# Output products by column halves, TensorE's program written out, sample's transfers in four parts

## The chip, the cores and the metric

The kernel runs on one core of one Trainium2 chip. Of the core's engines, TensorE (PE) multiplies matrices, VectorE (DVE) and ScalarE (ACT) work on rows, GpSimd (POOL) helps at the start, and SyncE (SP) issues most of the transfers; ACT issues some as well. Sixteen DMA engines move the data. The metric is the device time of one execution in microseconds (us), less is better.

## The reference

One layer of an encoder in 32-bit floats, for 256 prompt rows and 32 sample rows (288 tokens), width 1024:

```
mod = (silu(c) @ w_ada + b_ada)              # six modulation rows for each group
h   = rms_norm(x) * (1 + sc1) + sh1
proj = h @ w_in                              # 1024 -> 1536
a = pool_mix(proj[:, :512]);  b = conv_mix(proj[:, 512:])
merged = sigmoid(h@gate_w + gate_b), one half times a, the other times b
x   = x + g1 * (merged @ w_out)              # the output products
h2  = rms_norm(x) * (1 + sc2) + sh2
logits = h2 @ router_w + router_b;  top 4 of 32 experts, softmax over the four
gt = min(h2 @ Wg[e] + bg[e], 7);  up = clip(h2 @ Wu[e] + bu[e], -7, 7)
x   = x + g2 * sum_e weight[e] * ((gt * sigmoid(1.702*gt) * (up + 1)) @ Wd[e] + bd[e])
y   = rms_norm(x)                            # the last norm
```

Each of the 32 experts has three 1024 x 1024 matrices, 12.58 MB together.

## The kernel before

Prompt rows are two tiles of 128 partitions (t = 0, 1); the 32 sample rows are tile 2, kept as four strips of 32 partitions with a quarter of the columns each (`xs`). Every engine has its own program, written by hand; semaphores order them (`wait_ge`, `then_inc`), and an engine runs its program strictly in order.

SP first loads the prompt and the sample rows (L471, L472), then the front's weights piece by piece (L478) into a ring of 12 slots, and then expert weights in transfers of 2048 KB, six for each expert, into 10 pairs of slots; the first two experts' fill pairs as the front frees them (`piece_used`), and from then on a pair is loaded again when an item has used it (`refill`; whole pairs by L484, and the first and the last few in halves by L533). The first refill waits for the first item.

The front is the modulation, `w_in`, gates, pool and conv products (L1481 to L1630), some with short filling matmuls in PE's pauses (`fill`, L1388). Modulation rows go through memory: ACT stores them in `mod_rows` and loads them again spread over partitions, by `spread_sample` (L748) for the sample's four strips in one transfer.

Then come the output products (`out_part`, L1647), merged times `w_out`, in quarters q of 256 columns: tile 0's first half (q 0, 1), its second half, tile 1's first half, q 2, q 3. DVE adds each part to x (`add_output` and `add_prompt`, L1109 and L1112), PE transposes the new x (`turn`, L1656) for the logits of the router (L1661), ACT squares parts of it for the norm (L815 and on). `choose` on DVE finds the four best experts of each row; `early_ranks` (L1702 to L1707) counts rows of each expert with PE, and stands in the middle of the last quarter's product. `first_slots`, `ranked` and `mine` on DVE (L1147 to L1190) give each row its place; `second_gain` (L1197) prepares tile 1.

Then experts run in items of up to 64 row slots; 33 items are run here, so one expert has two. An item is a gate, an up and a down product (`product`, L1781: 32 matmul instructions each), with the scatter of the item before and the gather of the next between them; DVE and ACT apply bias and activation meanwhile. PE's program has a loop over six groups of five experts (L1881, the five bodies written out), then two more experts behind it, each body inside a loop over the expert's items (L1877). In the last experts the products wait for halves of a pair (`LAST_HALVES`): the down product's last quarter alone needs the very last load (L1777).

Of the kernel before, what the change touches and what calls it, by code (L numbers as in the profile page):

```python
# [21 lines left out]
ACT = mybir.ActivationFunctionType  # L22
# [3 lines left out]
D = 1024  # L26
# [12 lines left out]
E = 32  # L39
# [49 lines left out]
def build(nc, x_prompt, x_sample, state_pool, state_conv, c_prompt, c_sample, norm1_g, norm2_g, final_g,  # L89
# [3 lines left out]
    with ExitStack() as ctx:  # L93
# [356 lines left out]
        def strip(q):  # L450
            return slice(32 * q, 32 * q + NS_TOK)
# [9 lines left out]
        def quad_row(ap, r, at):  # L461

            return ap[r:r + 1, at:at + D].rearrange("a (q d) -> q a d", q=4).broadcast_to([4, NS_TOK, QUAD])

# [4 lines left out]
        def _(sp):  # L469
            for t in range(2):  # L470
                sp.dma_start(x[:, t, :], x_prompt[0, P * t:P * (t + 1), :]).then_inc(x_ld[t], 16)  # L471
            sp.dma_start(xs[:, :], x_sample[0].rearrange("n (q d) -> q n d", q=4)).then_inc(x_ld[2], 16)  # L472
            for f in range(N_FRONT):
                if f >= RING:
                    sp.wait_ge(piece_used, f - RING + 1)
                if FRONT[f][0] != "none":
                    src, dst = front_piece(f)
                    sp.dma_start(dst, src).then_inc(slot_ld[f % RING], 16)  # L478
# [178 lines left out]
        def _(act):  # L657
# [89 lines left out]
            def spread_sample(quads, b, at, done):  # L747
                act.dma_start(quads, quad_row(mod_rows[b], 1, D * at)).then_inc(done, 16)  # L748
# [69 lines left out]
            for hh in range(2):  # L818
                cs = slice(HALF * hh, HALF * (hh + 1))
                act.wait_ge(x2_ready, 2 + hh)  # L820
                a.activation(h2[:, 0, cs], x[:, 0, cs], ACT.Square, accum_out=stat[:, 12 + hh:13 + hh]).then_inc(ssq2, 1)
                if hh == 0:
                    act.wait_ge(x2_turned, 2)
                    a.activation(x2T[:, 0:4, :], bank[0][:, :].rearrange("p (k n) -> p k n", k=4), ACT.Copy).then_inc(x2T_act, 1)
# [4 lines left out]
            act.wait_ge(x2_ready, 4)  # L829
            a.activation(h2[:, 1, 0:HALF], x[:, 1, 0:HALF], ACT.Square, accum_out=stat[:, 14:15]).then_inc(ssq2, 1)  # L830
# [58 lines left out]
        def _(dve):  # L889
# [37 lines left out]
            dve.wait_ge(x_ld[2], 16)  # L927
# [186 lines left out]
            def add_prompt(t, cs, src, after):  # L1114
                add_output(x[:, t, cs], g1b[:, cs], src, part[:, cs.start % HALF:cs.start % HALF + cs.stop - cs.start], after)
# [38 lines left out]
            dve.wait_ge(spread_ld[0], 32)  # L1154
# [8 lines left out]
            dve.wait_ge(spread_ld[1], 64)  # L1163
# [3 lines left out]
            add_prompt(0, slice(HALF, D), bank[5][:, :], 2)  # L1167
            dve.wait_ge(logit_mm, 1)
            choose(2, 1)
            dve.wait_ge(ssq2, 3)  # L1170
            v.tensor_tensor(stat[:, 0:1], stat[:, 12:13], stat[:, 13:14], ALU.add).then_inc(mean2, 1)
            dve.wait_ge(x2_turned, 3)
# [4 lines left out]
            dve.wait_ge(wo_mm, 4)  # L1177
            add_prompt(1, slice(0, HALF), bank[7][:, :], 3)
            dve.wait_ge(wo_mm, 5)
            add_prompt(1, slice(HALF, HALF + 256), bank[2][:, 0:256], 4)  # L1180
# [13 lines left out]
            def second_gain(cs, after):  # L1194

                dve.wait_ge(x2_ready, after)
                v.tensor_tensor(h2[:, 1, cs], x[:, 1, cs], a2b[:, cs], ALU.mult).then_inc(gained, 1)  # L1197

            second_gain(slice(0, HALF), 4)
# [185 lines left out]
        def _(pe):  # L1385
# [13 lines left out]
            def first_rows(row):  # L1399

                for j in range(2):
                    mm(bank[4][32 * j:32 * j + 32, :], ada_sel[:, row + j, :], bada[:, :], start=True, stop=False,
                       skip_group_check=True)
# [42 lines left out]
            pe.wait_ge(ada_ld, 16)  # L1446
            first_rows(2)
            fill(12)
# [231 lines left out]
            out_part(bank[5][:, :], 0, 2, 2)  # L1680
# [5 lines left out]
            pe.wait_ge(sqrt_ready, 3)  # L1686
            out_part(bank[7][:, :], 1, 0, 2)
            pe.wait_ge(x2_ready, 3)
            turn(0, range(4, 8), bank[1]).then_inc(x2_turned, 1)
            out_part(bank[2][:, 0:256], 1, 2, 1, used_before=2)  # L1690
            pe.wait_ge(x2T_act, 1)
            pe.wait_ge(x2T_dve, 2)
            pe.wait_ge(logit_read, 1)
            logits(0, range(KD)).then_inc(logit_mm, 1)
            pe.wait_ge(x2_ready, 4)
            turn(1, range(4), bank[0]).then_inc(x2_turned, 1)
# [12 lines left out]
            out_part(bank[4][:, 0:256], 1, 3, 1, used_before=1, mid=early_ranks)  # L1709
# [5 lines left out]
            logits(1, range(4)).then_inc(piece_used, F_END - N_FRONT)  # L1715
            pe.wait_ge(x2_ready, 6)
# [157 lines left out]
            def expert(g, j, last=False):  # L1874
                e = g * TURN + j
                next_first = pe.value_load(base_i[0:1, bass.ds(e + 1, 1)], min_val=1, max_val=MAX_ITEMS)
                with pe.Fori(pe.snap(first_item, min_val=0, max_val=MAX_ITEMS), next_first) as n:  # L1877
                    item(n, g, j, last)
                pe.reg_mov(first_item, next_first)

            with nc.Fori(0, E // TURN, engines=[mybir.EngineType.PE], hint_back_edge=True) as g:  # L1881
                for j in range(TURN):
                    expert(g, j)
            for j in range(E % TURN):
                expert(E // TURN, j, last=(j == E % TURN - 1))
# [42 lines left out]
```

## Time and profile before

| | |
|---|---|
| runs, median of 3 | 1154.52 us (1154.15 to 1156.7) |
| profiled execution | 1156.52 us, span 1154.7 us |
| granted clock of PE, mean | 0.992 |
| busy: PE, DVE, ACT, POOL | 97%, 43%, 15%, 2% |
| moved by DMA | 456.19 MB, mean 395 GB/s |

The profile is of one execution. "Busy" is the share of the span in which an engine executes an instruction of its own; a granted clock of 1.00 is TensorE at 2.4 GHz, 0.50 at 1.2 GHz. A chain of waits is followed back from the last instruction to what released it; "issue" in it is time in which the engine waited for nothing that the profile shows. A timeline row has start, duration, engine, line, operation, and in brackets the idle time before it with what ended it.

### The profile page before, as it was taken

What the parts mean: (1) busy time and instruction counts of PE and PEld (TensorE: products, weight loads), DVE (VectorE), ACT (ScalarE), POOL (GpSimd) and SP (SyncE); (2) the same over time, 40 slices, a digit from 0 to 9 for tenths busy, and PEclk for the clock granted to TensorE, in tenths of its full rate; (3) what the DMA queues carried; (4) which work ended last, traced back from release to release, by engine and by line L of the source; (5) the groups of instructions that cost most, each with busy time, mean ns of one, the idle gap of its engine ahead of it and who ended that gap; (6) DMA issues with size and microseconds to landing.
All of it is one profiled execution on the core that took longest, in us unless ns stands there. A gap on an engine that the chain in (4) does not pass through costs nothing.

```text
span 1154.7 us, 15959 instructions
## 1 busy us (share of the span) xinstructions
PE 1125.1 (97%) x5950; PEld 459.6 (40%) x5951; DVE 492.6 (43%) x1133; ACT 179.0 (15%) x340; POOL 28.8 (2%) x78
## 2 busy tenths in 40 slices
PE   7999999999999999999999999999999999999896
PEld 4676676633333333333333333333333333333232
DVE  3299414654433443334443334333443343333244
ACT  4001301221111111111111111111111111111112
POOL 3000400000000000000000000000000000000000
PEclk9999999999999999999999999999999999999899
DMA  9977789899999999999999999999999999999993
GB/s 344 350 271 259 269 306 367 294 354 420 429 427 428 428 429 429 429 429 427 429 429 429 428 429 428 429 430 429 428 428 429 429 429 429 428 429 429 428 423 148
DMA packets 59505, 456.19 MB, mean 395 GB/s; under 512 B 7205, under 2 KB 26977, under 8 KB 31701
## 3 DMA queue, kind: packets, MB, share of 16 engines
q1 hardware_dynamic: 55108, 452.35, 94.9%
q10 hardware_dynamic: 4369, 3.47, 1.0%
q8 instruction: 18, 0.29, 0.1%
q14 instruction: 10, 0.08, 0.0%
HBM read 454.40 MB, written 1.40 MB: 395 GB/s over the span
## 4 chain that ended last, share of the span: by engine, by line
PE 82%; DMA 16%; DVE 1%; issue 0%; SPq 0%; DVEq 0%
PE bank L1781 49%; DMA arena<-in_exp_w_up 7%; PE bank L1560 5%; PE bank L1808 4%; PE bank L1507 4%; PE bank L1725 4%; DMA arena<-in_exp_w_gate 4%; DMA ring<-in_exp_w_gate 4%; PE bank L1647 2%; DMA ring<-in_w_in 2%; PE bank L1863 2%; PE bank L1733 1%; PE bank L1799 1%; PE bank L1630 1%; PE bank L1481 1%; PE bank L1737 1%
## 5 line engine op out<-in xcount | busy, mean ns | idle before, releaser
L1781 PE MATMUL bank<-ring,arena 128*64 128x512 f32 x1888 | 420.7, 598 | 8.6 <-DMA ring<-in_exp_w_gate 4.6
L1781 PE MATMUL bank<-arena 128*64 128x512 f32 x1280 | 283.2, 595 | 3.4 <-DMA arena<-in_exp_w_gate 3.2
L1781 PEld LDWEIGHTS bank<-ring,arena 128*64 128x64 f32 x1888 | 132.4, 137 | 277.3 <-issue 264.6
L1781 PEld LDWEIGHTS bank<-arena 128*64 128x64 f32 x1280 | 88.9, 137 | 184.3 <-issue 171.7
L850 ACT ACTIVATE arena<-arena 32x256 f32<-32x256 f32 x136 | 56.1, 412 | 421.6 <-DVE arena L1241 420.4
L1318 DVE TENSOR_SCALAR arena<-bank 128x512 f32<-128x512 f32 x33 | 22.8, 692 | 167.3 <-PE bank L1781 167.3
L1326 DVE TENSOR_SCALAR arena<-bank 128x512 f32<-128x512 f32 x33 | 22.8, 692 | 166.4 <-PE bank L1781 166.4
L1304 DVE TENSOR_TENSOR x<-x,bank 128x512 f32<-128x512 f32 x132 | 84.6, 682 | 13.0 <-PE bank L1808 13.0
L1340 DVE TENSOR_TENSOR arena<-bank,biases 128x512 f32<-128x512 f32 x66 | 42.5, 686 | 109.9 <-PE bank L1781 109.9
L859 ACT ACTIVATE arena<-arena 128x512 f32<-128x512 f32 x33 | 20.8, 629 | 354.0 <-DVE arena L1318 354.0
L1808 PE MATMUL bank<-arena 64*128 64x512 f32 x264 | 65.6, 615 | 0.0
L1560 PE MATMUL bank<-arena,ring 128*128 128x288 f32 x256 | 64.4, 409 | 0.0
L1725 PE MATMUL bank<-h,arena 128*64 128x512 f32 x268 | 63.3, 592 | 0.0
L1011 DVE SCALAR_TENSOR_TENSOR arena<-h,arena 128x318 f32<-128x318 f32 x120 | 55.5, 540 | 0.0
L1560 PEld LDWEIGHTS bank<-arena,ring 128*128 128x128 f32 x256 | 48.1, 190 | 17.1 <-issue 4.2
L1507 PE MATMUL bank<-arena,ring 128*128 128x288 f32 x192 | 50.3, 423 | 2.7 <-DMA ring<-in_w_in 2.7
L1507 PEld LDWEIGHTS bank<-arena,ring 128*128 128x128 f32 x192 | 37.8, 199 | 15.1 <-DMA ring<-in_w_in 2.8
L859 ACT ACT_TABLE_LOAD x33 | 42.3, 1283 | 0.6
L1737 PE MATMUL bank<-biases,mine 32*64 32x288 f32 x264 | 40.0, 414 | 0.0
L1808 PEld LDWEIGHTS bank<-arena 64*128 64x128 f32 x264 | 22.7, 186 | 42.3 <-issue 42.3
L1246 DVE COPY arena<-arena 32x256 f32<-32x256 f32 x136 | 38.4, 282 | 2.5
L1733 PE MATMUL bank<-biases,mine 32*64 32x512 f32 x136 | 37.4, 613 | 0.0
(323 smaller groups left out, 729.3 us busy)
## 6 DMA issues: line engine op xcount, KB each, us to landing
ring<-in_exp_w_up SPq DMA_DIRECT2D x38, 2048.0 KB, 29.8
ring<-in_exp_w_down SPq DMA_DIRECT2D x36, 2048.0 KB, 31.3
ring<-in_exp_w_gate SPq DMA_DIRECT2D x36, 2048.0 KB, 31.0
arena<-in_exp_w_gate SPq DMA_DIRECT2D x25, 2048.0 KB, 28.8
arena<-in_exp_w_up SPq DMA_DIRECT2D x24, 2048.0 KB, 27.9
arena<-in_exp_w_down SPq DMA_DIRECT2D x24, 2048.0 KB, 31.9
ring<-in_w_ada SPq DMA_DIRECT2D x24, 1024.0 KB, 10.3
ring<-in_gate_w SPq DMA_DIRECT2D x8, 1024.0 KB, 6.4
```

Source lines behind the costliest of these rows:

```text
L850: ins = a.activation(*square_moves(1, s, u), ACT.Copy)
L859: a.activation(gsig, gmin, ACT.Sigmoid, scale=ALPHA).then_inc(gsig_ready, 1)
L1011: ins = v.scalar_tensor_tensor(out=yc[:, c, :], in0=uc_ext[:, c, k:k + CW], scalar=tap, in1=yc[:, c, :], op0=ALU.mult, op1=ALU.add)
L1304: ins = v.tensor_tensor(x[:, t, cs], x[:, t, cs], scatter_bank(t, hh), ALU.add)
L1340: v.tensor_tensor(ysb[gg], bank[5][:, :], g2h[:, gg, :], ALU.mult).then_inc(y_ev, 1)
L1507: ins = mm(bank[n % 4][:, 0:TOK], w[:, k, P * (n % 2):P * (n % 2 + 1)], (hS if n < UNSHIFTED else hT)[:, k, :], start=(k == 0), stop=(n >= ...
L1560: ins = mm(bank[n % 4][:, 0:TOK], w[:, k, P * (n % 2):P * (n % 2 + 1)], hT[:, k, :], start=(k == 0), stop=(k == KD - 1))
L1725: ins = mm(bank[0][64 * hh:64 * hh + 64, :], oh[:, t, :], half_rows(h2[:, t, :], hh), start=start, stop=stop, skip_group_check=True)
L1733: mm(bank[3][out, :], mine[B_GATE, :], bias_rows[B_GATE, cs], start=True, stop=False, skip_group_check=True)
L1737: found = mm(bank[6 + i][out, 0:TOK], mine[LOOKUP, :], routedT[:, i, :], start=True, stop=True, skip_group_check=True)
L1781: ins = mm(out[64 * hh:64 * hh + 64, :], lhs(k), w[:, D * (k % 2) + HALF * hh:D * (k % 2) + HALF * (hh + 1)], start=(done is y_mm and k == ...
L1808: ins = mm(scatter_bank(t, hh), ohwT[64 * hh:64 * hh + 64, P * t:P * (t + 1)], ysb[0][64 * hh:64 * hh + 64, :], start=True, stop=True, ski ...
```

## The change

Five things change.

1. Output products. Both tiles' first half of the columns come first, then tile 0's second half, then tile 1's quarters; banks, semaphore counts and the order of DVE's additions and of ACT's squares follow. The logits and transposes that stood between them move: tile 0's logits stand in the middle of the last quarter, the ranks behind it. A fill of two is added by tile 1's logits.
2. PE's program for the experts has no loop over groups: all 32 bodies are written one behind the other; the loop over an expert's items stays.
3. The sample's rows are loaded in four transfers of 32 partitions, behind the first piece of the front instead of ahead of it; each `spread_sample` is four transfers.
4. A fill of 9 ahead of `first_rows(2)` takes the place of a fill of 12 behind it.
5. Waits on the semaphores of these transfers count to 64, 80 and 160 instead of 16, 32 and 64.

```
@@ -469,8 +465,10 @@
                 sp.dma_start(x[:, t, :], x_prompt[0, P * t:P * (t + 1), :]).then_inc(x_ld[t], 16)
-            sp.dma_start(xs[:, :], x_sample[0].rearrange("n (q d) -> q n d", q=4)).then_inc(x_ld[2], 16)
             for f in range(N_FRONT):
+                if f == 1:
+                    for q in range(4):
+                        sp.dma_start(xs[strip(q), :], quarter(x_sample[0], q)).then_inc(x_ld[2], 16)
                 if f >= RING:
@@ -745,7 +743,9 @@
-                act.dma_start(quads, quad_row(mod_rows[b], 1, D * at)).then_inc(done, 16)
+                for q in range(4):
+                    row = mod_rows[b][1:2, D * at + QUAD * q:D * at + QUAD * (q + 1)]
+                    act.dma_start(quads[strip(q), :], row.broadcast_to([NS_TOK, QUAD])).then_inc(done, 16)
@@ -815,19 +815,19 @@
-            for hh in range(2):
-                cs = slice(HALF * hh, HALF * (hh + 1))
-                act.wait_ge(x2_ready, 2 + hh)
-                a.activation(h2[:, 0, cs], x[:, 0, cs], ACT.Square, accum_out=stat[:, 12 + hh:13 + hh]).then_inc(ssq2, 1)
-                if hh == 0:
-                    act.wait_ge(x2_turned, 2)
-                    a.activation(x2T[:, 0:4, :], bank[0][:, :].rearrange("p (k n) -> p k n", k=4), ACT.Copy).then_inc(x2T_act, 1)
+            act.wait_ge(x2_ready, 2)
+            a.activation(h2[:, 0, 0:HALF], x[:, 0, 0:HALF], ACT.Square, accum_out=stat[:, 12:13]).then_inc(ssq2, 1)
+            act.wait_ge(x2_ready, 3)
+            a.activation(h2[:, 1, 0:HALF], x[:, 1, 0:HALF], ACT.Square, accum_out=stat[:, 14:15]).then_inc(ssq2, 1)
+            act.wait_ge(x2_turned, 2)
+            act.wait_ge(wo_mm, 4)
+            a.activation(x2T[:, 0:4, :], bank[0][:, :].rearrange("p (k n) -> p k n", k=4), ACT.Copy).then_inc(x2T_act, 1)
+            act.wait_ge(x2_ready, 4)
+            a.activation(h2[:, 0, HALF:D], x[:, 0, HALF:D], ACT.Square, accum_out=stat[:, 13:14]).then_inc(ssq2, 1)
...
-            act.wait_ge(x2_ready, 4)
-            a.activation(h2[:, 1, 0:HALF], x[:, 1, 0:HALF], ACT.Square, accum_out=stat[:, 14:15]).then_inc(ssq2, 1)
@@ -1160,24 +1160,24 @@
-            dve.wait_ge(spread_ld[1], 64)
+            dve.wait_ge(spread_ld[1], 160)
...
-            add_prompt(0, slice(HALF, D), bank[5][:, :], 2)
+            add_prompt(1, slice(0, HALF), bank[2][:, :], 2)
...
-            dve.wait_ge(ssq2, 3)
+            dve.wait_ge(wo_mm, 4)
+            add_prompt(0, slice(HALF, D), bank[5][:, :], 3)
+            dve.wait_ge(ssq2, 4)
...
+            dve.wait_ge(wo_mm, 5)
+            add_prompt(1, slice(HALF, HALF + 256), bank[3][:, 0:256], 4)
...
-            dve.wait_ge(wo_mm, 4)
-            add_prompt(1, slice(0, HALF), bank[7][:, :], 3)
-            dve.wait_ge(wo_mm, 5)
-            add_prompt(1, slice(HALF, HALF + 256), bank[2][:, 0:256], 4)
@@ -1444,8 +1444,8 @@
             pe.wait_ge(ada_ld, 16)
+            fill(9)
             first_rows(2)
-            fill(12)
             pe.wait_ge(cT_ready, 1)
@@ -1677,23 +1677,24 @@
             turn_sample(bank[3][:, 0:QUAD], xs).then_inc(x2_turned, 1)
-            out_part(bank[5][:, :], 0, 2, 2)
+            out_part(bank[2][:, :], 1, 0, 2)
             pe.wait_ge(x2_ready, 2)
...
             logits(2, range(KD)).then_inc(logit_mm, 1)
-            pe.wait_ge(sqrt_ready, 3)
-            out_part(bank[7][:, :], 1, 0, 2)
-            pe.wait_ge(x2_ready, 3)
+            out_part(bank[5][:, :], 0, 2, 2, used_before=2)
+            out_part(bank[3][:, 0:256], 1, 2, 1)
+            pe.wait_ge(x2_ready, 4)
             turn(0, range(4, 8), bank[1]).then_inc(x2_turned, 1)
-            out_part(bank[2][:, 0:256], 1, 2, 1, used_before=2)
-            pe.wait_ge(x2T_act, 1)
-            pe.wait_ge(x2T_dve, 2)
-            pe.wait_ge(logit_read, 1)
-            logits(0, range(KD)).then_inc(logit_mm, 1)
-            pe.wait_ge(x2_ready, 4)
-            turn(1, range(4), bank[0]).then_inc(x2_turned, 1)
+            def early_logits():
+                pe.wait_ge(x2T_act, 1)
+                pe.wait_ge(x2T_dve, 2)
+                pe.wait_ge(logit_read, 1)
+                logits(0, range(KD)).then_inc(logit_mm, 1)
+                turn(1, range(4), bank[0]).then_inc(x2_turned, 1)
@@ -1706,13 +1707,16 @@
-            out_part(bank[4][:, 0:256], 1, 3, 1, used_before=1, mid=early_ranks)
+            out_part(bank[4][:, 0:256], 1, 3, 1, used_before=1, mid=early_logits)
+            pe.wait_ge(sqrt_ready, 3)
+            early_ranks()
             pe.wait_ge(x2_ready, 5)
...
             logits(1, range(4)).then_inc(piece_used, F_END - N_FRONT)
+            fill(2, bank[2])
             pe.wait_ge(x2_ready, 6)
@@ -1871,18 +1875,15 @@
             pe.wait_ge(base_ready, 1)
-            def expert(g, j, last=False):
-                e = g * TURN + j
-                next_first = pe.value_load(base_i[0:1, bass.ds(e + 1, 1)], min_val=1, max_val=MAX_ITEMS)
+            def expert(e, last=False):
+                g, j = e // TURN, e % TURN
+                next_first = pe.value_load(base_i[0:1, e + 1:e + 2], min_val=1, max_val=MAX_ITEMS)
                 with pe.Fori(pe.snap(first_item, min_val=0, max_val=MAX_ITEMS), next_first) as n:
...
-            with nc.Fori(0, E // TURN, engines=[mybir.EngineType.PE], hint_back_edge=True) as g:
-                for j in range(TURN):
-                    expert(g, j)
-            for j in range(E % TURN):
-                expert(E // TURN, j, last=(j == E % TURN - 1))
+            for e in range(E):
+                expert(e, last=(e == E - 1))
             items = pe.value_load(base_i[0:1, E:E + 1], min_val=E, max_val=MAX_ITEMS)
```

The order of instructions, as each program has them (line, operation, output and inputs, partitions x columns; `x8` is eight alike). First PE of the kernel before, at the output products behind tile 0's first half; `bank` is the accumulator, `ring` the weights, L1656 the transposes of x, L1661 the logits:

```order
L1647 MATMUL bank<-ring,arena 128x512 x8
L1656 MATMUL bank<-ident,x 128x128 x4
L1647 MATMUL bank<-ring,arena 128x256 x8
L1661 MATMUL bank<-arena 128x32 x8
L1656 MATMUL bank<-ident,x 128x128 x4
L1647 MATMUL bank<-ring,arena 128x256 x4
L1702 MATMUL bank<-rt,upto 128x32
L1703 MATMUL bank<-rt,ones 32x32
L1704 MATMUL bank<-rt,upto 32x32
L1706 MATMUL bank<-rt,ones 128x32
L1707 MATMUL bank<-rt,ones 128x32
L1647 MATMUL bank<-ring,arena 128x256 x4
```

The same place of PE in the changed kernel (its ranks are L1703 to L1708):

```order
L1647 MATMUL bank<-ring,arena 128x512 x8
L1647 MATMUL bank<-ring,arena 128x256 x8
L1656 MATMUL bank<-ident,x 128x128 x4
L1647 MATMUL bank<-ring,arena 128x256 x4
L1661 MATMUL bank<-arena 128x32 x8
L1656 MATMUL bank<-ident,x 128x128 x4
L1647 MATMUL bank<-ring,arena 128x256 x4
L1703 MATMUL bank<-rt,upto 128x32
L1704 MATMUL bank<-rt,ones 32x32
L1705 MATMUL bank<-rt,upto 32x32
L1707 MATMUL bank<-rt,ones 128x32
L1708 MATMUL bank<-rt,ones 128x32
```

The first of tile 1's two single quarters has moved ahead of a group of transposes, tile 0's logits and tile 1's first transposes into the middle of the last quarter, and the five matmuls of the ranks behind it.

DVE at the same place, as the difference from before (-) to after (+); L1109 and L1112 are the two operations of an addition to x, and the rows behind the last line choose tile 0's experts:

```order
-L1171 TENSOR_TENSOR stat<-stat 128x1
-L1173 COPY arena<-bank 128x4x128
-L1175 RECIPROCAL stat<-stat 128x1
+L1109 TENSOR_TENSOR arena<-bank,arena 128x512
+L1112 TENSOR_TENSOR x<-x,arena 128x512
+L1173 TENSOR_TENSOR stat<-stat 128x1
+L1109 TENSOR_TENSOR arena<-bank,arena 128x256
+L1112 TENSOR_TENSOR x<-x,arena 128x256
+L1177 COPY arena<-bank 128x4x128
+L1179 RECIPROCAL stat<-stat 128x1
```

Both additions now come ahead of tile 0's norm instead of behind it; the slots and the addition of the last quarter stand behind all of these as before.

PE of the kernel before at the end of the loop over groups (L1881); `base_i` holds each expert's first item:

```order
L1781 MATMUL bank<-arena 64x512 x16
L1877 REGISTER_ALU
L1877 COMPARE_AND_BRANCH
L1879 ISA
L1881 COMPARE_AND_BRANCH
L1876 TENSOR_LOAD base_i
L1876 ISA x2
L1877 ISA
L1877 UNCONDITIONAL_BRANCH
L1877 ISA
L1781 MATMUL bank<-ring,arena 64x512 x16
```

PE of the changed kernel between two experts:

```order
L1785 MATMUL bank<-ring,arena 64x512 x16
L1881 REGISTER_ALU
L1881 COMPARE_AND_BRANCH
L1880 TENSOR_LOAD base_i
L1880 ISA x2
L1881 ISA
L1881 UNCONDITIONAL_BRANCH
L1881 ISA
L1785 MATMUL bank<-arena 64x512 x16
```

The branch of the loop over groups is gone, and with it the hint at its head; the branch of the loop over an expert's items stands at each expert as before.

## Rows read from the trace of the kernel before

**Rows 1.** The page, part 1 (busy time) and part 3 (DMA queues).

```profile
PE 1125.1 (97%) x5950; PEld 459.6 (40%) x5951; DVE 492.6 (43%) x1133; ACT 179.0 (15%) x340; POOL 28.8 (2%) x78
...
q8 instruction: 18, 0.29, 0.1%
```

**Rows 2.** Stretches: us; PE, PEld, DVE, ACT, POOL; granted clock; DMA share; GB/s.

```profile
233.40:603.60 370.20, 370.20 (x1986) 127.49 (x1986) 151.67 (x336) 53.10 (x93) 0.00 (x0) 1.00 1.00 422
603.60:1079.70 476.10, 468.07 (x2482) 158.74 (x2481) 184.99 (x398) 70.85 (x125) 0.00 (x0) 1.00 1.01 429
1079.70:1094.70 15.00, 11.06 (x34) 3.08 (x34) 1.67 (x7) 0.00 (x0) 0.00 (x0) 0.77 1.01 427
```

**Rows 3.** The chain that ended last, two items: start us, us, what.

```profile
253.47 13.88 PE bank L1781 x64
...
280.41 13.88 PE bank L1781 x64
```

**Rows 4.** The chain that ended last, around 1080 us and at its end.

```profile
1079.71 1.90 PE bank L1781 x6
1081.61 3.93 issue
1085.54 9.18 PE bank L1781 x26
...
1134.71 7.04 PE bank L1781 x32
```

**Rows 5.** Waits of PE, whole span: us in total, times, longest.

```profile
PE bank L1781 <- issue: 3.9, 1, 3.9
```

**Rows 6.** The last two loads of weights (L533): issue, and time to landing.

```profile
L533 SPq DMA_DIRECT2D ring<-in_exp_w_down x2: 3612/3896/4180, 1097.9 to 1101.7; - x2
...
DMA to landing us min/median/max: 32.4/32.8/33.2
```

**Rows 7.** Start: the first piece (L478) alone, then timeline of SP, then of PE.

```profile
L478 SPq DMA_DIRECT2D ring<-in_w_ada x1: 432/432/432, 2.5 to 2.5; - x1
...
DMA to landing us min/median/max: 7.9/7.9/7.9
...
4.58 8.89 SPq L478 DMA_DIRECT2D ring<-in_w_in  x2
...
24.83 10.55 PE L1507 MATMUL bank<-arena,ring 128*128 128x288 f32 x32 [2.65 <-DMA ring<-in_w_in]
```

**Rows 8.** Busy time by stretch at the start (columns as in Rows 2).

```profile
0.00:10.40 10.40, 8.28 (x47) 7.00 (x48) 2.78 (x17) 5.64 (x11) 7.17 (x33) 1.00 0.82 289
24.00:30.00 6.00, 5.17 (x11) 3.74 (x12) 0.69 (x4) 0.00 (x0) 0.00 (x0) 0.50 1.04 408
```

**Rows 9.** Timeline of PE and then DVE at the output products and the routing.

```profile
220.55 0.30 PE L1702 MATMUL bank<-rt,upto 128*128 128x32 f32 x2
...
221.81 1.99 PE L1647 MATMUL bank<-ring,arena 128*128 128x256 f32 x8
...
207.09 0.48 DVE L1125 SCALAR_TENSOR_TENSOR arena<-xs,stat,biases 128x256 f32<-128x256 f32 x1 [7.70 <-DMA arena<-mod_rows]
...
221.32 0.54 DVE L1147 TENSOR_SCALAR arena<-slot,bank,rt 128x64 f32<-128x64 f32 x2 [0.90 <-PE bank L1704]
...
222.08 1.01 DVE L1197 TENSOR_TENSOR h<-x,arena 128x512 f32<-128x512 f32 x2
223.84 0.42 DVE L1109 TENSOR_TENSOR arena<-bank,arena 128x256 f32<-128x256 f32 x1 [0.75 <-PE bank L1647]
```

**Rows 10.** Timeline of SP: the freed pair of slots, and the first refills.

```profile
213.82 0.33 SPq L484 DMA_DIRECT2D ring<-in_exp_w_up  x1
...
235.30 6.53 SPq L533 DMA_DIRECT2D ring<-in_exp_w_down  x4
```

**Rows 11.** L748 on ACT (ns min/median/max), and the ACT timeline at 191 us.

```profile
L748 ACTq DMA_DIRECT2D biases<-mod_rows x2: 547/552/556, 158.7 to 173.1; - x2
...
191.52 0.42 ACT L815 ACTIVATE arena<-xs 128x256 f32<-128x256 f32 x1 [11.06 <-DVE xs L1112]
```

More of the change, by code:

```diff
@@ L459, in turned_sample @@
             return ap.rearrange("p (c q n) -> p c q n", c=2, q=4)
-        def quad_row(ap, r, at):
-            return ap[r:r + 1, at:at + D].rearrange("a (q d) -> q a d", q=4).broadcast_to([4, NS_TOK, QUAD])
         block = ctx.enter_context(nc.Block())
@@ L926, in _ @@
             v.tensor_scalar(h2[:, 0, :], x[:, 0, :], stat[:, 4:5], None, ALU.mult).then_inc(xn_ready, 1)
-            dve.wait_ge(x_ld[2], 16)
+            dve.wait_ge(x_ld[2], 64)
             step(v.tensor_tensor(squares, xs, xs, ALU.mult))
@@ L1152, in ranked @@
                 return v.tensor_tensor(routed[0:r, 0, t, 0:E], src[0:r, :], rt[0:r, 3, t, :], ALU.mult)
-            dve.wait_ge(spread_ld[0], 32)
+            dve.wait_ge(spread_ld[0], 80)
             dve.wait_ge(wo_mm, 1)
@@ L1197, in second_gain @@
                 v.tensor_tensor(h2[:, 1, cs], x[:, 1, cs], a2b[:, cs], ALU.mult).then_inc(gained, 1)
-            second_gain(slice(0, HALF), 4)
+            second_gain(slice(0, HALF), 3)
             second_gain(slice(HALF, HALF + 256), 5)
```

## The prediction, made without the result

> **What bounds the kernel now.** I read the page's busy shares first, then three stretches, then the chain that ended last, then single waits. TensorE (PE) is busy 97% of the span [rows 1], which invites the reading that everything is bound by PE. The stretches correct it [rows 2]. From 233.4 to 603.6 us PE is busy in every microsecond while the DMA engines already move 422 GB/s; from 603.6 to 1079.7 DMA stands at a share of 1.01 and 429 GB/s, and PE is idle 476.10 - 468.07 = 8.0 us. So the expert phase starts bound by PE, which lives on weights loaded ahead, and ends bound by the weights. One expert's three matrices are 6 x 2048 KB = 12.58 MB, or 12.58/429 = 29.3 us of transfer, against 26.94 us of PE for an item (280.41 - 253.47) [rows 3]. Three points then fix the end: when the first slots are refilled (235.30 [rows 10], tied to the first item's start), how many bytes follow, and what PE still does after the last weights land.
>
> At that last point there is slack. The last two loads are issued at 1097.9 and 1101.7, and take 32.4 to 33.2 us [rows 6], so the last lands at about 1101.7 + 32.4 = 1134.1. PE's last product is 32 matmuls from 1134.71 for 7.04 us [rows 4], to 1141.75. Only its last quarter (1.76 us) needs the last load (the wait of L1777); PE is thus late by 1141.75 - (1134.1 + 1.76) = 5.9 us. The chain names the cause: at 1081.61 PE waits 3.93 us for "issue", and its next 26 matmuls take 9.18 us [rows 4], where 26 x 13.88/64 = 5.64 is normal [rows 3]; the stretch's granted clock is 0.77 [rows 2], so part of it ran at the 1.2 GHz level after that idle. It is the one such wait on "issue" in the span [rows 5], and it lies just where the loop over six groups of five experts (L1881) is left and the code behind it begins. Together PE loses 3.93 + 3.54 = 7.5 us, of which 5.9 survive to the end.
>
> Durations come from the profiled run, 1156.5 us (span 1154.7 and 1.8 around it), 2.0 above the median of 1154.5; I carry the difference over to the median.
>
> **Writing out TensorE's program.** The loop, its branch and its exit go; experts follow each other in straight code. Removed: the one stall. Then PE ends 1.76 us behind the last landing: -5.9. Bounds: 0, if the stall only moves to another place where PE is late, and -7.5, if all that PE loses counts. I take -5.9, because the landing stops the gain there.
>
> Added: instructions to be fetched. The trace has 18 transfers on the instruction queue [rows 1]. PE executes 5950 + 5951 = 11,901 instructions [rows 1]; an item has 1986/(370.2/26.94) = 144.5 matmuls [rows 2, 3], say 144, with as many weight loads 288. Seven bodies were written, five in the loop and two behind it, for 33 items (one expert has two), so 26 passes ran code that was there already: 11,901 - 26 x 288 = 4413 instructions in 18 blocks, 245 a block. Now only the second item re-uses code: 11,901 - 288 = 11,613, or 47.4 blocks, 29.4 more. The 18 blocks took 0.1% of 16 x 1154.7 = 18.5 engine-us, 1.03 us each [rows 1]; 29.4 more, spread over 16 engines of a saturated stretch, are 29.4 x 1.03/16 = +1.9 us. Bounds: 0, if blocks fill gaps, and 29.4 x 1.03 = +30.3, if each falls on the same engine, for which every 2 MB load then waits. I take 1.9: the first turn of the loop, five items from 233 us on, ran code for the first time too, at an unchanged 26.94 us an item, PE without a gap, and 422 GB/s [rows 2, 3].
>
> A rule of the Trainium skill bears on this ("Runtime: NRT & Kernel Launch", Instruction fetch mechanics): instructions come in blocks of 16 KiB ahead of a sequential stream, and a taken branch out of a short window stalls until its target is fetched, so straight code is to be preferred. 0.29 MB/18 = 16 KB agrees. But by that rule the loop's taken back edges, whose body is five items long, should have stalled too, five times 3.93 us; the trace has one such wait, at the exit [rows 5]. By the rule the gain would be the same here, since earlier stalls would lie in a stretch that transfers bound.
>
> **Output products by halves of the columns, both tiles each.** The same products, additions and transposes run in another order, on PE and on VectorE (DVE). In the middle of the last quarter's product PE used to run the ranks (from 220.55); its second half began at 221.81 and ended at 223.80 [rows 9]. Now logits stand there and the ranks behind the product. Without the ranks, 221.81 - 220.55 = 1.26 us, the product ends at 222.54. The slots on DVE start 0.77 behind the ranks (221.32 against 220.55), so at 223.31, and with what follows up to 223.09 take 1.77 us [rows 9]. The last quarter's addition, queued behind them on DVE, then starts at 225.1 instead of 223.84: +1.2, which goes on through norm and gather to the first item. Bounds: -1.3 (DVE is no longer late and the product is early by all of 1.26) and +2.5 (twice my sum, if logits in the middle wait for their DVE copy as well). I take +1.2. The wait of 7.70 us for the sample's scale row at 207.09 [rows 9] may vanish with the split transfer; PE was busy then, so 0, unless choosing for the sample was late for the ranks, which they show no sign of. One column half of the product frees its ring slots a product earlier, but at 213.82 a freed pair only lets a queued load in [rows 10]; the DMA queue is full before and behind it, so 0.
>
> **Sample's transfers in four parts.** Three spreads of four ACT issues each instead of one add nine issues of 0.55 us, 5.0 us of ACT [rows 11], beside an ACT that idles 11.06 us before 191.52 [rows 11]: 0 (bound +5.0, if that cover is gone). The load of the sample's rows moves behind the first front piece on SP, three more issues ahead of pieces. SP runs ahead of the queue, with an issue that blocks from 4.58 for 8.89 us [rows 7], so issuing costs 0.
>
> What it may gain is at the start. The first piece, issued at 2.5, landed at 10.4 [rows 7], when 10.4 us x 289 GB/s = 3.0 MB had moved [rows 8], though only 1.05 (prompt) + 0.13 (sample) + 1.05 (piece) = 2.23 MB lay ahead. The 0.77 MB too much, at 408 GB/s [rows 8], are 1.9 us in which some DMA engines were done and others late; the sample's rows, one transfer with an outer dimension of four, are a candidate. PE's first dense product waits 2.65 us for its piece at 24.83 [rows 7] and runs at half the clock, the 1.2 GHz level, from 24 to 30 [rows 8], which costs 5.17/2 = 2.6 of its busy time. Bounds: 0, and -(2.65 + 2.6) = -5.2. I take -1.2, nearer to the lag's 1.9 than to 0, and not all of it, since it is shared with the first piece and what the other queues load. The fills, 9 ahead of the first rows instead of 12 behind them and 2 more at the logits, stand where PE waits for data: 0 (bound by the nearest short matmuls, 0.30 for two [rows 9]).
>
> The Trainium skill has a rule that speaks against this ("DMA: Bandwidth & Descriptors", its table of advice): two transfers to disjoint halves of the partitions serialize, and one transfer over all is better. Its section on why a DMA increments its semaphore by 16 states the reverse for this shape: the slowest dimension sets how many engines take part, here 4. By the first, this term is 0 and the time 1151.7; by the second, an estimate, four engines carry 0.13/4 - 0.13/16 = 0.025 MB too much each, 1.0 us at 408/16 GB/s. The rows show the lag but not whose it is.
>
> **Sum.** -5.9 + 1.9 + 1.2 - 1.2 = -4.0: 1152.5 by the profiled run, 1150.5 by the median.
>
> **Rivals.**
> 1. The front gains its whole bound: the piece comes 2.65 us earlier and the clock does not fall. For it: both the wait and the half clock are in the rows. Against: no row shows which load is late. -4.0 - (5.2 - 1.2) = -8.0: 1146.5.
> 2. The stall stays: PE's program still has an inner loop for each expert's items, and leaving one may cost what leaving the outer one did, late enough to count. Against: 32 such exits cost nothing [rows 5]. 0 + 1.9 + 1.2 - 1.2 = +1.9: 1156.4.
> 3. Slower: fresh code costs. Each of the 29.4 new blocks delays one DMA engine that the next load waits for, and nothing is made up: +30.3 instead of +1.9, -4.0 + 28.4 = +24.4, 1178.9. Without blocks the sum is -5.9, so it makes the kernel slower once more than 5.9/29.4 = 0.20 of a block's 1.03 us remains. Against: the first turn of the loop. The same side is reached if the routing takes its +2.5 and the tail gains nothing.
>
> **Chances.** Forecast 0.57, own range 1148.5 to 1152.5; front 0.17; stall stays 0.16; slower 0.10. What a measurement of this kernel tells from no change is 0.2%, 2.3 us: faster is under 1152.2, slower over 1156.8. The forecast gives 0.50 to faster and 0.07 to same; the first rival faster; the second 0.12 to same and 0.04 to slower. Together 0.67, 0.19, 0.14. The range, 1146 to 1156, leaves out the third rival and the upper half of the second.
>
> **What would show it.** No wait of PE on "issue" after 1000 us, PE ending about 1.8 us behind the last landing, about 47 instruction transfers, first item's start about unchanged (+1.2 - 1.2), and 429 GB/s kept. A new wait on "issue", a throughput under 425, or a first item more than 3 us away from 233.4 would make it wrong.

## The result: 0.33% slower, and the profile after

The changed kernel takes 1157.25 us (median of 20 runs, 1155.23 to 1163.94) against 1154.32 of the kernel before in the same comparison (20 runs): a ratio of 1.0033, 95% interval 1.0020 to 1.0046. Forecast was 1150.5, clearly faster. By the ratio it is slower by about 3.8 us; the two medians differ by 2.9.

The profiled run has a span of 1156.3 us, 1.6 above that of before. The page's busy row and its row of the instruction queue [rows 1] now read:

```profile
PE 1123.4 (97%) x5948; PEld 459.0 (40%) x5948; DVE 492.7 (43%) x1133; ACT 179.5 (16%) x340; POOL 28.8 (2%) x78
...
q8 instruction: 48, 0.79, 0.3%
```

Thirty more blocks were fetched: 29.4 was the estimate. The stretches [rows 2], same columns:

```profile
233.40:603.60 370.20, 369.06 (x1970) 126.62 (x1974) 150.61 (x333) 52.56 (x93) 0.00 (x0) 1.00 1.00 420
603.60:1079.70 476.10, 463.85 (x2472) 157.88 (x2458) 183.21 (x393) 67.67 (x119) 0.00 (x0) 1.00 1.01 428
1079.70:1094.70 15.00, 13.29 (x62) 4.19 (x58) 3.98 (x13) 3.35 (x6) 0.00 (x0) 1.00 1.00 426
```

PE now idles 476.10 - 463.85 = 12.3 us where it idled 8.0, and the long stretch moves 428 GB/s instead of 429. The chain's end [rows 4] shows what replaced the stall (`ring` and `arena` are the places in on-chip memory that hold the weights):

```profile
1071.73 44.06 DMA arena<-in_exp_w_gate
1115.93 7.09 PE bank L1785 x32
1123.02 1.92 PE bank L1812 x8
...
1136.22 7.04 PE bank L1785 x32
```

No "issue" stands there any more. The last item starts at 1115.93, when its gate weights land, after 44.06 us of a chain of transfers, and runs without a gap to 1136.22 + 7.04 = 1143.26; before, PE was done at 1141.75. Waits of PE have no row on "issue" [rows 5]; the two longest rows are waits for gate weights:

```profile
PE bank L1785 <- DMA ring<-in_exp_w_gate: 8.5, 10, 1.2
PE bank L1785 <- DMA arena<-in_exp_w_gate: 5.0, 6, 1.1
```

The last loads [rows 6] and the first refill [rows 10] in the changed kernel, each from its own view (issue and landing of one line; SP's timeline):

```profile
L531 SPq DMA_DIRECT2D ring<-in_exp_w_down x2: 2952/3274/3595, 1107.3 to 1111.0; - x2
...
DMA to landing us min/median/max: 29.9/30.4/30.9
```

```profile
234.63 3.77 SPq L531 DMA_DIRECT2D ring<-in_exp_w_down  x3
```

So the last load lands at 1111.0 + 29.9 = 1140.9. From the first refill to there it takes 1140.9 - 234.63 = 906.3 us; before, 1134.1 - 235.30 = 898.8. The same bytes of weights came 7.5 us later.

Why is not in a row but in the stamps of the landings. The trace keeps one for each of the sixteen parts of a load. How far the first and the last part of a load lie apart (us), read from those stamps for the load that lands nearest to the time at the head:

```
landing near (us)     250   400   600   800  1000  1090
before                1.2   2.4   2.4   2.4   2.4   2.4
changed               0.8   3.5   5.1   6.6   8.1   9.7
```

And the sixteen parts of one load near 1100 us, in us ahead of its last one. Before:

```
-2.35 -2.35 -2.31 -2.23 -2.17 -2.05 -1.97 -1.95 -1.84 -1.72 -1.70 -0.47 -0.27 -0.07 -0.03  0
```

Changed:

```
-9.67 -9.58 -9.48 -9.46 -9.35 -9.32 -9.29 -9.19 | -3.49 -2.83 -2.59 -2.34 -2.07 -1.94 -1.45  0
```

Eight parts are still early and together; the other eight have fallen 6 to 10 us behind. The slowest fell back in five steps of 1.5 to 1.7 us, seen in the loads that landed at 287, 465, 672, 855 and 1042 us. The trace also dates the packet of each block of TensorE's program. Those at 283.0, 460.7, 668.4, 852.2 and 1040.4 us, 2 to 5 us ahead of these five landings, are exactly every eighth block. The seven between them move other late parts: with each block from 300 to 1100 us the distances to the first part grow by 1.0 to 1.8 us together, 1.5 on the mean, and nearly all of it among the eight. So a block sets one part back, and the blocks go round eight parts. A load is complete with its last part, so PE waits for the slowest: the parts of the last item's gate weights land from 1106.1 to 1115.8 us, and PE starts at 1115.93.

The front and the routing, each answered by a view of the changed kernel: the first piece (L476) [rows 7], PE's first dense product, PE and then DVE at the output products and the first item [rows 9].

```profile
L476 SPq DMA_DIRECT2D ring<-in_w_ada x1: 426/426/426, 1.7 to 1.7; - x1
...
DMA to landing us min/median/max: 7.5/7.5/7.5
```

```profile
22.92 10.92 PE L1507 MATMUL bank<-arena,ring 128*128 128x288 f32 x32 [1.65 <-DMA ring<-in_w_in]
```

```profile
188.84 7.13 PE L1647 MATMUL bank<-ring,arena 128*128 128x512 f32 x16
...
220.72 0.30 PE L1703 MATMUL bank<-rt,upto 128*128 128x32 f32 x2
...
232.65 7.09 PE L1785 MATMUL bank<-ring,arena 128*64 128x512 f32 x32
```

```profile
221.49 0.53 DVE L1147 TENSOR_SCALAR arena<-slot,bank,rt 128x64 f32<-128x64 f32 x2 [0.77 <-PE bank L1705]
...
223.18 0.41 DVE L1109 TENSOR_TENSOR arena<-bank,arena 128x256 f32<-128x256 f32 x1
```

For comparison, two rows of PE of the kernel before that were not shown:

```profile
190.40 7.13 PE L1647 MATMUL bank<-ring,arena 128*128 128x512 f32 x16
...
233.33 7.09 PE L1781 MATMUL bank<-ring,arena 128*64 128x512 f32 x32
```

The first piece lands at 1.7 + 7.5 = 9.2 instead of 10.4; the first dense product starts 1.9 us earlier, the output products 1.56 earlier. From there to the first item it takes 232.65 - 188.84 = 43.81 instead of 42.93, so the first item starts 0.68 earlier.

### The profile page after: what moved, and what is told of

It reads as the page before. It is cut to its first block, busy times and chain, and to the rows that moved or that the text cites. A ratio compares the mean times of both kernels' runs of the same rounds, so it can differ in the third digit from the quotient of the medians.

```text
span 1156.3 us, 15872 instructions
## 1 busy us (share of the span) xinstructions
PE 1123.4 (97%) x5948; PEld 459.0 (40%) x5948; DVE 492.7 (43%) x1133; ACT 179.5 (16%) x340; POOL 28.8 (2%) x78
## 4 chain that ended last, share of the span: by engine, by line
PE 78%; DMA 20%; DVE 1%; SPq 0%; issue 0%; DVEq 0%
PE bank L1785 46%; DMA ring<-in_exp_w_gate 8%; PE bank L1560 5%; PE bank L1507 4%; PE bank L1812 4%; PE bank L1729 4%; DMA arena<-in_exp_w_gate 4%; DMA arena<-in_exp_w_up 4%; DMA ring<-in_exp_w_up 4%; PE bank L1647 2%; DMA ring<-in_w_in 1%; PE bank L1867 1%; PE bank L1737 1%; PE bank L1630 1%; PE bank L1803 1%; PE bank L1481 1%
## 5 line engine op out<-in xcount | busy, mean ns | idle before, releaser
L1785 PE MATMUL bank<-ring,arena 128*64 128x512 f32 x1888 | 418.1, 595 | 10.4 <-DMA ring<-in_exp_w_gate 8.5
```

Source lines behind the costliest of these rows:

```text
L1785: ins = mm(out[64 * hh:64 * hh + 64, :], lhs(k), w[:, D * (k % 2) + HALF * hh:D * (k % 2) + HALF * (hh + 1)], start=(done is y_mm and k == ...
```

## The experiments

Twelve kernels, compared with the kernel before on the same chip; a ratio is followed by its 95% interval. Runs of one kernel differ by up to 12.5 us (one run of the kernel before that took 4089 us is left out of the ratios). The record lists each run's mean granted clock, from 0.984 to 0.998, and among the runs of a kernel 0.001 of it goes with about 1 us. So I read ratios with their intervals, and in the profiles distances that start behind the front: from the first output product to the first item, and from the first refill to the last landing.

**Loop put back.** In the changed kernel:

```
-            for e in range(E):
-                expert(e, last=(e == E - 1))
+            with nc.Fori(0, E // TURN, engines=[mybir.EngineType.PE], hint_back_edge=True) as g:
+                for j in range(TURN):
+                    expert(g, j)
+            ...
```

> The changed kernel with the loop over six groups of five experts put back into TensorE's program; all else as changed. Theory F (instruction fetches: the written-out program's blocks fall on a few DMA engines, and the slowest sixteenth of each load lands up to 7 us later): the number of instruction transfers falls from 48 to about 18, the last weights land as in the kernel before less the 0.7 us by which the first item starts earlier, the wait on issue of 3.9 us returns near 1081 us, and the time is about 1153.6 (0.9994 of before). Rival R (the other parts of the change make the loads late): the last landing stays near 1141, the time near 1157 or above.

Measured: 0.9999 (0.9973 to 1.0026), 18 instruction transfers, parts 2.3 us apart, first refill to last landing 899.2 us. The stall is back in the chain:

```profile
1078.21 1.94 PE bank L1785 x8
1080.14 4.45 issue
1084.59 8.04 PE bank L1785 x24
```

The other parts of the change don't make the loads late. Rival R is out.

**Written out, nothing else.** In the kernel before:

```
-            with nc.Fori(0, E // TURN, engines=[mybir.EngineType.PE], hint_back_edge=True) as g:
-            ...
+            for e in range(E):
+                expert(e, last=(e == E - 1))
```

> The kernel before with TensorE's program written out for all experts and nothing else changed. Theory F: about 48 instruction transfers, last landing 7 us later than before, no wait on issue, time about 1157.9 (1.003). Rival R: the stall goes and nothing else comes, 1154.3 - 5.9 = 1148.4 (0.995).

Measured: 1.0044 (1.0019 to 1.0070), parts 9.8 us apart near 1090, first refill to last landing 906.0 us; no wait on "issue". Page row and chain:

```profile
q8 instruction: 48, 0.79, 0.3%
```

```profile
1069.07 45.08 DMA arena<-in_exp_w_gate
1114.28 7.09 PE bank L1781 x32
```

As theory F has it, by itself and in size: against the kernel before, the program written out costs 0.0044 of 1154 us, 5.1 us, and the changed kernel against the one with the loop put back 0.0034, 3.9 us, each give or take some 3 us. Both fit 7.5 us of late loads less a stall of 2.4 to 3.6 us.

**Loop left one turn earlier.** In the changed kernel with the loop put back:

```
-            with nc.Fori(0, E // TURN, ...
+            with nc.Fori(0, E // TURN - 1, ...
...
-            for j in range(E % TURN):
-                expert(E // TURN, j, last=(j == E % TURN - 1))
+            for e in range(E // TURN * TURN - TURN, E):
+                expert(e // TURN, e % TURN, last=(e == E - 1))
```

> The changed kernel with a loop over five groups of five experts, and seven experts written out behind it, so that the loop is left near 930 us instead of 1080. Theory F: the exit's wait of 3.9 us stands where PE waits for weights anyhow and is made up by the end; about 6 more instruction transfers than with the loop over six groups cost some 1.4 us; time about 1149.1 (0.9955). Rival R: near 1157.

Measured: 1.0002 (0.9978 to 1.0026); 24 instruction transfers, parts 2.2 apart and 3.8 at the end, first refill to last landing 899.9. The profile does what was expected, a span of 1150.0 with the wait moved to where it is made up:

```profile
935.68 2.27 issue
...
1065.41 44.04 DMA arena<-in_exp_w_gate
1109.59 7.09 PE bank L1785 x32
```

But over the runs the time did not fall by 0.45%. That was the first sign that the stall at the loop's exit is worth less than the profiled run of before made it.

**Loop without its hint.** In the changed kernel with the loop put back:

```
-            with nc.Fori(0, E // TURN, engines=[mybir.EngineType.PE], hint_back_edge=True) as g:
+            with nc.Fori(0, E // TURN, engines=[mybir.EngineType.PE]) as g:
```

> The changed kernel with the loop over six groups of five, without the hint at its back edge. Theory F with a fetch that simply runs on in order: each of the five taken back edges costs PE 3.9 us, made up by the end, and the exit costs nothing; about 10 more instruction transfers, +2.5 us on the last landing; time about 1150.2 (0.9965). If the hint changes nothing: as with the loop and its hint, about 1153.6. Rival R: near 1157.

Measured: 0.9985 (0.9960 to 1.0011); 18 instruction transfers, parts 2.2 to 2.4 apart, first refill to last landing 898.8, no wait on "issue" anywhere, at a back edge or at the exit. It is not the expected mixture but simpler: the five bodies stay, none is fetched again, and the code behind is there in time. The trace's packets of the instruction queue date each block: here one more block than with the hint comes in the loop's first turn, at 346.0 us. In the kernel with the loop and its hint no block comes between 323.2 and 1082.2 us, and the one at 1082.2 falls into the wait at the exit (1080.14 to 1084.59). The chain's end:

```profile
1063.34 44.18 DMA arena<-in_exp_w_gate
1107.66 7.09 PE bank L1785 x32
...
1127.97 7.04 PE bank L1785 x32
```

PE ends at 1135.01, 2.5 us behind the last landing of 1132.5.

**GpSimd's program made longer, first try.** In the kernel without the hint, at the end of its program:

```
+            spare = pool.alloc_register("spare")
+            pool.reg_mov(spare, 0)
+            for i in range(1, 31):
+                pool.wait_ge(y_ev, 2 * i)
+                for _ in range(256):
+                    pool.reg_add(spare, spare, 1)
```

> The kernel without the hint (loop over six groups kept, all other parts as changed), with 30 x 256 register additions written out at the end of GpSimd's program, one batch for each item, which nobody waits for. Theory F (the fetched blocks themselves make the loads late): instruction transfers rise from 18 to about 48, the sixteenths of a late load land some 10 us apart instead of 2.4, the last expert's gate weights come 7 us later, and the time is 7 us over the kernel without the hint, about 1.0045 of before. Rival U (it is something in TensorE's written-out program, not the fetch): GpSimd's additions cost nothing, 0.9985 as without them.

Measured: 0.9998 (0.9979 to 1.0016), 18 transfers. GpSimd's own instruction queue (q14) moved 10 packets, as without the additions: they did not make the fetched program longer, so this tells nothing of the fetch. It repeats the kernel without the hint, and shows how far two comparisons of it lie apart.

**The kernel before without the hint.** The edit of the kernel without the hint, in the kernel before (`hint_back_edge=True` out).

> The kernel before without the hint at the loop's back edge, nothing else. If the tail's term was sized right, the wait on issue near 1081 goes, TensorE follows the last landing by 1.8 us or starts its last item as soon as the gate weights are there, and the time falls by up to 5.9 us: 0.995. If other runs of the kernel before lose less there than the profiled one, or the loop then waits elsewhere: 0.998 to 1.000.

Measured: 0.9983 (0.9965 to 1.0002). The span of its profile is 1146.2, no wait on "issue". The full -5.9 (0.995) lies outside the interval. The best estimate of what the stall costs on average is some 2 us; the interval, 4.0 us faster to 0.2 slower, does not tell it from nothing. Other profiles with the hint show why: the wait at the exit is 3.9 us in the run of before, 4.5 with the loop put back, 2.3 with the loop left early, and in the next two experiments 0.7 and 5.1.

**Sample's transfers in four parts, nothing else.** In the kernel before, the change's lines for `xs` (L472), `spread_sample` (L748) and the counts waited for (64, 80, 160).

> The kernel before with the sample's transfers in four parts (load of the rows behind the first piece, three spreads of four), nothing else. The prediction's term: first dense product of TensorE starts about 1.2 us earlier than 24.83, time 0.999. Rival (one transfer is as good as four): starts at 24.8, time 1.000.

Measured: 0.9994 (0.9974 to 1.0015), unclear. In its profile the first dense product starts at 22.46, where 23.6 was expected and 24.83 was before; over all ten profiles with the split it starts at 21.66 to 24.32, mean 22.6, and in the four without (before, written out only, before without hint, order only) at 23.70 to 24.83, mean 24.2. The load is both split and moved behind the first piece; no run separates the two. The wait at the loop's exit, here and in the next experiment:

```profile
PE bank L1781 <- issue: 0.7, 1, 0.7
```

```profile
PE bank L1785 <- issue: 5.1, 1, 5.1
```

**Output products by column halves, nothing else.** In the kernel before, the change's lines from `out_part(bank[2][:, :], 1, 0, 2)` to `fill(2, bank[2])`, with DVE's and ACT's order that goes with them.

> The kernel before with the output products by column halves (TensorE's, VectorE's and ScalarE's order), nothing else. The prediction's term: from the first output product to the first item 42.93 + 1.2 = 44.1 us, time 1.001. Rival (the new order saves the ranks' detour as well): 41.6, time 0.999.

Measured: 1.0029 (1.0007 to 1.0052), slower by more than its term. First output product to first item is 48.9 us here, since the clock fell in the routing (stretch of 35 us, columns as in the rows of stretches):

```profile
200.00:235.00 35.00, 34.50 (x177) 22.62 (x176) 20.22 (x65) 8.32 (x22) 0.00 (x0) 0.85 0.77 289
```

**GpSimd's program made longer, second try.** In the kernel without the hint:

```
+            for i in range(1, 31):
+                pool.wait_ge(y_ev, 2 * i)
+                for _ in range(256):
+                    pool.sem_inc(chain_p, 1)
```

> The kernel without the hint (loop over six groups kept, other parts as changed), with 30 x 256 semaphore increments at the end of GpSimd's program, a batch for each item; nobody waits for them, but they make its program 30 blocks of 16 KB longer. (The register additions tried before were removed by the compiler.) Theory F (fetched blocks themselves make the loads late): about 30 more instruction transfers, the sixteenths of a late load some 10 us apart instead of 2.4, the last expert's gate weights 7 us later, 1.0045 of before. Rival U (it is something else in TensorE's written-out program): nothing changes, 0.9985 to 0.9998 as without them.

Measured: 1.0351 (1.0326 to 1.0376). GpSimd's program comes over another queue in packets of 8 KB, 60 more of them; the page's rows and PE's two longest waits:

```profile
q14 instruction: 70, 0.57, 0.1%
q8 instruction: 18, 0.29, 0.1%
```

```profile
PE bank L1790 <- DMA ring<-in_exp_w_gate: 18.5, 17, 1.3
PE bank L1790 <- DMA arena<-in_exp_w_gate: 12.7, 11, 1.2
```

Near 1090 us one part of a load is 28.9 us behind the first, and the other fourteen lie within 1.7 us of the first: here all blocks fall on one engine. First refill to last landing is 935.0 us, 36 more. Nobody waits for GpSimd there, and TensorE's program is a loop of 18 transfers: the fetch by itself makes the loads late. Its size was far off, 0.0351 where 0.0045 was expected: where the blocks go decides.

**Groups of ten.** In the kernel without the hint:

```
-            with nc.Fori(0, E // TURN, engines=[mybir.EngineType.PE]) as g:
-                for j in range(TURN):
-                    expert(g, j)
+            with nc.Fori(0, E // TURN // 2, engines=[mybir.EngineType.PE]) as two:
+                for j in range(2 * TURN):
+                    expert(two * 2 + j // TURN, j % TURN)
```

> The kernel without the hint, its loop over three groups of ten experts instead of six of five. Written out, an expert's body is 19.8 KB (from the two programs' sizes), so ten are 198 KB. Theory F with code that stays only if the loop's body is small: the ten don't stay, each turn fetches them again, about 48 instruction transfers and the loads 7 us late, 1.0033 as with all written out. If they stay: about 24 transfers, 1.0 us late, 0.999.

Measured: 1.0069 (1.0042 to 1.0095). Ten bodies don't stay: 52 transfers, parts 9.6 us apart, first refill to last landing 906.5; and PE waits on "issue" at 504.5 and 807.2 us, where the two back edges are taken, which five bodies never did:

```profile
q8 instruction: 52, 0.85, 0.3%
```

```profile
PE bank L1785 <- issue: 6.9, 2, 3.5
```

**Two edits together.** The kernel before without the hint and with the sample's transfers in four parts, as in the two experiments on these.

> The kernel before without the hint at the back edge and with the sample's transfers in four parts: the two edits that were faster by themselves (0.9983 and 0.9994). Theory F and the parts' independence: 0.9977. Rival (the front's gain is lost, since its runs differ by more): 0.9985.

Measured: 0.9989 (0.9970 to 1.0008), median 1148.3: the lowest of all medians, not told apart from before by the interval, which holds both the 0.9977 of theory F and the rival's 0.9985.

**Fills behind the ranks.** In the kernel without the hint:

```
             early_ranks()
+            fill(4, bank[2])
             pe.wait_ge(x2_ready, 5)
```

> The kernel without the hint, with four short filling matmuls behind the ranks. In the profiles with the new order of output products the granted clock fell to 0.50 in the routing in five of eight (first output product to first item 45.4 or 49 us instead of 43.8), with the old order in none of five (42.9). Theory C (PE's sparse work behind the last dense product lets the clock fall): with the fills it stays, 43.8 to 44.2 us in the profile, and the runs' mean clock rises from 0.993 to about 0.995, the time to about 0.9975 of before. Rival (the fall has nothing to do with what PE does there): mean clock 0.993, 0.9985 to 0.9998 as without the fills, or slower by the fills.

Measured: 0.9979 (0.9956 to 1.0001); mean clock of its runs 0.9952 against 0.9931 without the fills, first output product to first item 44.2 us. The routing's stretch keeps its clock:

```profile
200.00:235.00 35.00, 34.77 (x205) 23.23 (x205) 20.95 (x74) 9.42 (x22) 0.00 (x0) 1.00 0.74 275
```

This fits theory C but does not show it. Three of eight profiles without these fills kept the clock too, the other comparison of the kernel without the hint (GpSimd, first try) has a mean clock of 0.9943, and the intervals of the ratios (0.9985, 0.9998 and 0.9979) overlap.

The distance from first refill to last landing, over all fourteen profiles:

```
18 or 24 instruction transfers (10 kernels)     898.5 to 899.9 us
48, 48 and 52                                   906.2, 906.0, 906.5
18, and GpSimd's 60                             935.0
```

## Why the prediction was wrong

- "29 more over 16 engines of a saturated stretch", +1.9: this step failed. The number of blocks was right (30). But a block is carried by one engine, the parts of later loads are not shifted to the others, and the blocks went round eight of the sixteen: +7.5 us in the pair of profiles, 0.25 us a block. This is rival 3's mechanism, which had one chance in ten. By its own sum it turns the kernel slower from 0.20 us a block on; it holds at a quarter of its price of 1.03. The evidence I set against it, an unchanged 26.94 us an item and 422 GB/s in the loop's first turn, could not show a lag: PE lived on weights loaded ahead there, and five or six blocks had only begun to spread the parts, from 1.2 to 2.4 us. The row to read was the time to landing, not the throughput. None of the three signs that were to show the forecast wrong came up (no wait on "issue", 428 GB/s, the first item 0.7 us away), because none of them looks at a landing. And the threshold should have warned me: a sum of -4 that a fifth of a bound can turn is no clear forecast.
- "The stall goes", -5.9: right in the pair of profiles, where PE ends 2.4 us instead of 7.7 behind the last landing, -5.3. Over the runs it is mis-sized: without the hint the kernel before gains some 2.0 us (0.9983, interval to 1.0002), and the two pairs with and without the loop give 2.4 and 3.6 if 7.5 is taken for the late loads. The wait differs from run to run, 0.7 to 5.1 us, and one profiled run was taken for all.
- Its cause was placed right, but the remedy is smaller than writing all out: without the hint the loop shows no stall at all. I had not thought of the hint.
- Output products, +1.2: +0.88 in the profile (43.81 against 42.93), by the steps foreseen; the slots start 221.49 - 220.72 = 0.77 behind the ranks, and the last addition starts 0.90 later against the first output product (223.18 - 188.84 = 34.34, before 223.84 - 190.40 = 33.44). Not foreseen was the clock: in five of the eight profiles of the new order run first, it fell to the 1.2 GHz level in the routing, and 45.4 us (three) or 49 (two) passed instead of 43.8; with the old order in none of five (42.9). PE had by then ended its last dense product and was doing short ones with waits between. The order by itself cost 1.0029 (1.0007 to 1.0052). Beside the two edits together, old order and no hint at 0.9989, the new order without the hint has 0.9985 and 0.9998, so the size of this cost is not settled.
- Sample and fills, -1.2: the first piece lands 1.2 us earlier, as written; the output products 1.56. Right in the profiles; the runs (0.9994) do not tell it from nothing.
- Sum by the pair of profiles: -5.3 + 7.5 + 0.88 - 1.56 = +1.5, and the spans differ by 1.6. Over the runs, with -2.0 for the stall, about +4.8 where +3.8 (2.3 to 5.3) was measured. That sum leaves out the clock's fall, 1.9 us on the mean of the eight profiles, and the three parts measured alone (1.0044, 1.0029, 0.9994) add up to 1.0067. So the runs carry the sign and the fetch as its cause, but not each term to better than some 3 us.

The page "Runtime: NRT & Kernel Launch" of the Trainium skill (Instruction fetch mechanics) would write code out. Its statement on blocks of 16 KiB agrees with the trace (0.79 MB in 48); here straight code cost 7.5 us, and the loop without a hint neither stalled nor, after its first turn, fetched.

## What to carry to other kernels

Where the end is set by saturated loads, count the instruction blocks fetched beside them as transfers on single DMA engines: one late sixteenth delays a whole load, and nothing evens it out. Keep the loop if its body stays resident, and look at how far the parts of a load lie apart, not at GB/s. A stall seen in one profile is one draw; where it varies, look at several runs before crediting its removal.

## What was unexpected of the hardware

- An expert's body is 20 KB of TensorE's program (0.79 - 0.29 = 0.50 MB for 25 more bodies). Five of them, 100 KB, stayed over six turns without a fetch behind the first turn; ten, 200 KB, did not, and each taken back edge then cost 3.5 us.
- The hint at the back edge is what made the exit stall: five profiles with it have a wait of 0.7 to 5.1 us at the exit, the seven loops without it none there. With it the block behind the loop was fetched at the exit (1083.2 us in the kernel before), without it in the first turn (344.3 us in the kernel before without the hint).
- A block of TensorE's program set the engine that carried it back by about 1.5 us, though its own packet took 1.07 on the mean; why more than the packet is open. GpSimd's blocks came in 8 KB packets, and by the landings all on one engine, 28.9 us by 60 packets.
- Which eight engines carry TensorE's blocks the trace does not say; that they are eight is read from the landings and from the slowest part's step with every eighth block.
